# Gated-delta inverse on two stacked 64x64 diagonal blocks instead of one 128x128 block

## What is computed

```python
decay = jnp.exp(jnp.where(causal, g[..., :, None] - g[..., None, :], -jnp.inf))
Lmat = jnp.where(strict, jnp.einsum('bhncd,bhnmd->bhncm', kb, k) * decay, 0.0)
rhs = jnp.concatenate([vb, kb * jnp.exp(g)[..., None]], axis=-1)
sol = lax.linalg.triangular_solve(Lmat, rhs, left_side=True, lower=True, unit_diagonal=True)
```

## Time and profile before

| | |
|---|---|
| median of 3 runs | 4148.92 us (4146.3 to 4148.97) |
| profiled execution, its span | 4149.6 us |
| stage `gdn_core`, from the first product of level 0 to the first product of the recurrence | 348.63 to 486.24 us |
| TensorE busy over the span | 97% |

### The profile page before, as it was taken

The page is one execution under the profiler, slowest core; times in us unless marked ns, Lnnn a source line. Parts: engine busy times, 40 slices in busy tenths (PEclk is TensorE's granted clock), DMA queues, the critical chain, the costliest instruction groups (busy, mean ns, idle before and its releaser), DMA issues. The chain is left out here.

```text
span 4149.6 us, 54482 instructions
## 1 busy us (share of the span) xinstructions
PE 4030.1 (97%) x19995; PEld 3172.1 (76%) x19995; DVE 2112.4 (51%) x3948; ACT 828.9 (20%) x1835; POOL 1337.1 (32%) x1034
## 2 busy tenths in 40 slices
PE   7999999999999999999999999999999999999998
PEld 3888958887886588866688648888766787478887
DVE  3776534422553433226448535785344486357852
ACT  2432210001333200004321202111133301111110
POOL 1334304444320144421137201444311263004543
PEclk9999999999999999999999999999999999999999
DMA  7222224324440232352223231233442133313232
GB/s 241 71 61 76 61 79 130 101 86 134 126 143 21 87 91 81 87 120 60 64 60 86 74 99 51 81 91 86 96 84 64 44 88 86 84 49 91 81 86 76
DMA packets 622999, 360.81 MB, mean 87 GB/s; under 512 B 68778, under 2 KB 592331, under 8 KB 622324
## 3 DMA queue, kind: packets, MB, share of 16 engines
q1 hardware_dynamic: 607944, 335.85, 30.0%
q10 hardware_dynamic: 14892, 22.78, 1.7%
HBM read 344.41 MB, written 6.82 MB: 85 GB/s over the span
## 5 line engine op out<-in xcount | busy, mean ns | idle before, releaser
L847 PE MATMUL psum<-h_normed,weight_slot 128*128 128x256 f32 x2624 | 594.9, 380 | 0.0
L847 PEld LDWEIGHTS psum<-h_normed,weight_slot 128*128 128x128 f32 x2624 | 499.5, 190 | 69.1 <-issue 1.0
L755 POOL TENSOR_TENSOR weight_slot<-weight_slot 128x512 f32<-128x512 f32 (+1 forms) x130 | 177.2, 1363 | 886.6 <-DMA weight_slot<-in_w_ffn_in 291.6
L947 DVE COPY work<-psum 128x256 f32<-128x256 f32 x98 | 41.1, 420 | 598.2 <-PE psum L847 598.2
L3569 PE MATMUL psum<-sums_of_h,weight_slot 128*128 128x256 f32 x1280 | 282.8, 379 | 0.0
L3569 PEld LDWEIGHTS psum<-sums_of_h,weight_slot 128*128 128x128 f32 x1280 | 243.2, 190 | 33.1
L847 PE MATMUL psum<-sums_hidden,weight_slot 128*128 128x256 f32 x1056 | 244.0, 379 | 0.5 <-POOL weight_slot L761 0.3
L847 PE MATMUL psum<-sums_in,weight_slot 128*128 128x256 f32 x1008 | 231.3, 379 | 0.0
L847 PE MATMUL psum<-sums_of_h,weight_slot 128*128 128x256 f32 x960 | 221.0, 380 | 4.0 <-POOL weight_slot L761 4.0
L3569 PE MATMUL psum<-h_normed,weight_slot 128*128 128x256 f32 x960 | 217.6, 383 | 5.3 <-PEq L205 5.3
L847 PEld LDWEIGHTS psum<-sums_hidden,weight_slot 128*128 128x128 f32 x1056 | 200.3, 190 | 29.0 <-POOL weight_slot L761 2.0
(11 more groups left out here) (591 smaller groups left out, 7238.5 us busy)
## 6 DMA issues: line engine op xcount, KB each, us to landing
weight_slot<-in_w_ffn_in SPq DMA_DIRECT2D x88, 512.0 KB
weight_slot<-in_ffn_w_up SPq DMA_DIRECT2D x88, 512.0 KB
weight_slot<-in_w_gate SPq DMA_DIRECT2D x64, 512.0 KB
weight_slot<-in_w_in SPq DMA_DIRECT2D x40, 512.0 KB, 5.6
weight_slot<-in_dsw_w_in SPq DMA_DIRECT2D x36, 512.0 KB, 6.6
weight_slot<-in_gdn_w_in SPq DMA_DIRECT2D x32, 512.0 KB, 15.3
weight_slot<-in_w_ffn_out SPq DMA_DIRECT2D x64, 256.0 KB
tile_ahead<-in_w_ada SPq DMA_DIRECT2D x16, 1024.0 KB, 5.2
```

Source lines behind the costliest of these rows:

```text
L755: nc.gpsimd.tensor_tensor(b(self.S1), b(self.A21), b(self.A22), ALU.add).then_inc(self.folded, 1)
L847: last = nc.tensor.matmul(c.ps[:, 4 * bank + r // 2, (r % 2) * self.HALF:(r % 2 + 1) * self.HALF], c.slots[s][:, b * 512 + k * P:b * 512 + ...
L947: nc.vector.tensor_copy(u4, p(self.P1)).then_inc(self.link, 1)
```

## The change

Until the last level the matrices are block diagonal, with blocks of at most 64. The change stores the two diagonal 64x64 blocks of a chunk one above the other (partitions 0 to 63 and 64 to 127, 64 columns), so that T and U of a head take 256 columns each and stand side by side in one tile `tu` of 512. Every 128x128 product of levels 0 to 4 becomes a pair of 64x64 products, block 0 on partitions 0 to 63 to PSUM partitions 0 to 63 and block 1 on 64 to 127 to 64 to 127, in the same PSUM bank. Y and Z of a head go into one bank, so VectorE updates T and U with one instruction. At level 4 Y is formed for block 0 only, and U is written out in full 128x128 form, whose left half GpSimd has set to zero. Level 5 forms only the 64x64 block off the diagonal, with single 64x64 products, from `lt` without a mask, and VectorE writes its negative.

The masks have 64 columns instead of 128; masks, pairs and the result banks have four buffers instead of two. In `gdn_heads` the instruction that writes `lt` becomes two, of 64x512 and 64x256 elements. The hardware loops of levels 1 to 4 are written out. The 32 rows of side work are spread over 40 slots (slots 4 to 43) instead of 32.

```diff
-                nc.vector.tensor_tensor(st["lt"][:, ds(n, 1), :], c.ps[:, 4, :], flat, ALU.mult).then_inc(freed, 1)
+                nc.vector.tensor_tensor(near, made[0:HC, :, :], decay[0:HC, :, :], ALU.mult)
+                nc.vector.tensor_tensor(far[:, :, 0:HC], made[HC:P, :, HC:P], decay[HC:P, :, HC:P], ALU.mult).then_inc(freed, 1)
...
             def mask(i, h):
-                pool.wait_ge(x_done, i * GH + (h + 1))
-                nc.gpsimd.tensor_tensor(tiles(masked[:, h % 2, :]), tiles(st["lt"][:, h, :]),
-                                        levels[:, ds(i + 1, 1), :].to_broadcast([P, TT, P]), ALU.mult).then_inc(mask_ready, 1)
+                j = i * GH + h
+                if j >= 4:
+                    pool.wait_ge(x_done, j - 3)
+                nc.gpsimd.tensor_tensor(tiles(mask_of[h % 4]), lower[:, h, :, 0:HC],
+                                        levels[:, i + 1:i + 2, :].to_broadcast([P, TT, HC]), ALU.mult).then_inc(mask_ready, 1)
...
-                for t in range(TT):
-                    at = slice(t * P, (t + 1) * P)
-                    last = nc.tensor.matmul(c.ps[:, h % 2, at], masked[:, h % 2, at], tt[:, h, at], start=True, stop=True)
+                for t, at in enumerate(CHUNKS):
+                    if i < LAST:
+                        for b in BLOCKS:
+                            last = nc.tensor.matmul(c.ps[b, h % 2, at], mask_of[h % 4][b, at], tu[b, h, 0, at], start=True, stop=True)
+                    else:
+                        last = nc.tensor.matmul(c.ps[HC:P, h % 2, at], lower[0:HC, h, t, HC:P], tu[0:HC, h, 0, at], start=True, stop=True)
...
+                if i < LAST:
+                    for at in CHUNKS:
+                        for b in BLOCKS[0:1] if i == LAST - 1 else BLOCKS:
+                            nc.tensor.matmul(c.ps[b, bank, at], tu[b, h, 1, at], x[b, at], start=True, stop=True)
+                    for t, at in enumerate(CHUNKS):
+                        for b in BLOCKS:
+                            last = nc.tensor.matmul(c.ps[b, bank, W + t * HC:W + (t + 1) * HC], x[b, at], tu[b, h, 1, at], start=True, stop=True)
+                else:
+                    for t, at in enumerate(CHUNKS):
+                        last = nc.tensor.matmul(c.ps[0:HC, bank, at], x[HC:P, at], full[HC:P, h, t, HC:P], start=True, stop=True)
...
-                nc.vector.tensor_tensor(tt[:, h, :], tt[:, h, :], c.ps[:, 2 + h % 2, :], ALU.subtract).then_inc(t_ready, 1)
...
+                if i < LAST - 1:
+                    both = tu[:, h, :, :].rearrange("p a n -> p (a n)")
+                    nc.vector.tensor_tensor(both, both, c.ps[:, bank, :], ALU.subtract).then_inc(tu_ready, 1)
```

More of the change, by code:

```diff
@@ L82, in constant_tables @@
     levels = []
-    for lv in range(LEVELS):
-        same = (row >> (lv + 1)) == (col >> (lv + 1))
-        levels.append(same & ((col >> lv) & 1 == 1) & ((row >> lv) & 1 == 0))
-    t["levels"] = np.concatenate(levels, 1) * 1.0
+    near, far = row % HC, col[:, :HC]
+    for lv in range(LEVELS - 1):
+        same = (near >> (lv + 1)) == (far >> (lv + 1))
+        levels.append(same & ((far >> lv) & 1 == 1) & ((near >> lv) & 1 == 0))
+    t["levels"] = np.concatenate(levels + [near == far], 1) * 1.0
     t["chunkmask"] = ((row // GC == col // GC) & (row <= col)) * 1.0
@@ L1683, in head @@
                 nc.vector.tensor_tensor(st["qk"][:, ds(n, 1), :], c.ps[:, 7, :], flat, ALU.mult)
-                nc.vector.tensor_tensor(st["lt"][:, ds(n, 1), :], c.ps[:, 4, :], flat, ALU.mult).then_inc(freed, 1)
+                made = c.ps[:, 4, :].rearrange("p (t n) -> p t n", t=TT)
+                near, far = (st["lt"][half, ds(n, 1), :].rearrange("p a (t n) -> p (a t) n", t=TT) for half in (slice(0, HC), slice(HC, P)))
+                nc.vector.tensor_tensor(near, made[0:HC, :, :], decay[0:HC, :, :], ALU.mult)
+                nc.vector.tensor_tensor(far[:, :, 0:HC], made[HC:P, :, HC:P], decay[HC:P, :, HC:P], ALU.mult).then_inc(freed, 1)
             dve.wait_ge(c.x_kept, 16)
@@ L1698, in _, with gdn_core @@
             head(GH - 1, 1, False)
[L1701 removed]
+def gdn_core(c, layer, st, tu, uu):
     nc = c.nc
@@ L1726, in gdn_core @@
         LAST = LEVELS - 2
+        BLOCKS = (slice(0, HC), slice(HC, P))
+        W = TT * HC
+        CHUNKS = [slice(t * HC, (t + 1) * HC) for t in range(TT)]
+        mask_of = [masked[:, b // 2, (b % 2) * W:(b % 2 + 1) * W] for b in range(4)]
+        pair_of = [pairs[:, b // 2, (b % 2) * W:(b % 2 + 1) * W] for b in range(4)]
+        inner_of = [inner[:, b, 0:W] for b in range(2)]
+        lower = st["lt"][:, :, :].rearrange("p h (t n) -> p h t n", t=TT)
+        full = uu.rearrange("p h (t n) -> p h t n", t=TT)
+        PAIRS_AHEAD, ADA_FROM, ADA_SLOTS = 3, 4, 40
         def tiles(ap):
@@ L1765, in _ @@
                 mask(0, h)
-                if h + 3 < GH:
-                    pair(h + 3)
-            for i in range(1, LAST + 1):
+                if h + PAIRS_AHEAD < GH:
+                    pair(h + PAIRS_AHEAD)
+            for i in range(1, LAST):
                 for h in range(GH):
                     mask(i, h)
+                if i == 1:
+                    nc.gpsimd.memset(full[:, :, :, 0:HC], 0.0).then_inc(cleared, 1)
         @block.tensor
         def _(pe):
-            pe.sem_inc(x_done, 2)
             pe.sem_inc(out.done, 2)
@@ L1832, in _ @@
             turn(1)
-            for h in range(GH + 1):
-                if h < GH:
-                    inner_product(0, h, True)
-                if h >= 1:
-                    outer_products(0, h - 1, True, True)
-                if h + 2 < GH:
-                    turn(h + 2)
-            with pe.Fori(1, LAST) as i:
+            for i in range(LAST):
                 for h in range(GH + 1):
@@ L1844, in _ @@
                     if h >= 1:
-                        outer_products(i, h - 1, True, False)
+                        outer_products(i, h - 1)
+                    if i == 0 and h + 2 < GH:
+                        turn(h + 2)
             for h in range(GH + 2):
@@ L2021, in scale_row @@
                     dve.sem_inc(taken, 1)
-            for h in range(3):
+            for h in range(PAIRS_AHEAD):
                 start(h)
-            for h in range(GH):
-                if h + 3 < GH:
-                    start(h + 3)
-                level(0, h, True)
-            assert LAST - 1 == ADA_LATE and GH == KT
-            with dve.Fori(0, LAST - 1) as i:
-                for h in range(GH):
-                    level(i, h, True, 1)
-                    scale_row(i, h)
-            for h in range(GH):
-                level(LAST, h, False)
+            ROWS = KT * ADA_LATE
+            for j in range((LAST + 1) * GH):
+                i, h = j // GH, j % GH
+                if i == 0 and h + PAIRS_AHEAD < GH:
+                    start(h + PAIRS_AHEAD)
+                level(i, h)
+                j -= ADA_FROM
+                if 0 <= j < ADA_SLOTS:
+                    for r in range(j * ROWS // ADA_SLOTS, (j + 1) * ROWS // ADA_SLOTS):
+                        scale_row(r // KT, r % KT)
             at, b = 4 * (ADA_FIRST + ADA_ROWS), c.column("b_ada")
```

110 lines of the change are left out of this document (56 added, 54 removed).

## The result

The changed kernel takes 4116.61 us (median of 4 runs, 4114.11 to 4117.96), the one before 4148.38 us (4 runs, 4146.3 to 4148.97): a ratio of 0.9924 with an interval of 0.9911 to 0.9936. It is faster, by 31.8 us (0.8%), where 57 were forecast. The time lies above the range (4084 to 4109).

The account below looks back on a forecast made before the run. TensorE was taken to bound the kernel. First product to recurrence: 15.0 + 35.1 + 12.4 + 21.3 = 83.8 us against 137.6, 53.8 less; with 3.6 at the start, 57.4 gained: 4092 us, range 4084 to 4109.

Parts of the forecast that it names:

- The batch: TensorE, 64x64 products: 16 records in overlapping pairs at 0.06 us a pair, 0.48 us a batch.
- Rival B: TensorE batches: pairs don't overlap or records come no faster, 0.93 us a batch, 4144 us in all; chance 0.12.
- Levels 1 to 3 ... TensorE-bound: Levels 1 to 3: TensorE sets the pace at 1.44 us a slot, 24 slots and 0.5 making 35.1 us.
- Each half of the 1 MB loads is ... hidden: Levels 1 to 3: each half of the loads lands in 5.1 us and is used up in 7 us.
- Level 4, 12.4 us: Level 4: VectorE sets the pace at 1.55 us a slot against TensorE's 1.42; eight slots take 12.4 us.
- Rival A: Inverse: VectorE or a latency sets the pace, slots 1.6 us, 1.9 in level 4; 4103 us in all; chance 0.13.
- Level 5, 21.3 us: Level 5 and tail: single 64x64 products at 0.46 us a batch, 0.2 a slot for size changes; 21.3 instead of 26.5.
- rival C: Whole inverse: the clock falls to 1.2 GHz with the array half used and more short waits; 4168 us, slower; chance 0.04.
- Start, 3.6 us gained: Before the first product: half-size GpSimd operations and half the masks loaded bring it to 345.0; 3.6 us gained.
- The rest: The recurrence and all later stages: same work, no wait on anything that moved, zero change.

Follow-up runs that it names:

- before_unrolled: The kernel before the change with its hardware loop over levels 1 to 4 written out, nothing else: 4146.46 us, ratio 0.9998.
- one_load: The changed kernel with only the first two of the eight 1 MB loads of modulation weights: 4108.11 us, ratio 0.9903.
- warm: The changed kernel with eight dummy 128x128 products by 512 columns on TensorE before the first product with the keys: 4106.3 us, ratio 0.9895.
- split: The changed kernel with one side row a slot in levels 1 to 3, none in level 4, eight in level 5: 4108.03 us, ratio 0.9905.
- grouped: The changed kernel with each batch's four products of block 0 issued first, then block 1's four, instead of in turn: 4116.54 us, ratio 0.9925.
- loops_split: The changed kernel with the edits of loops and split together: 4097.05 us, ratio 0.9875.
- loops: The changed kernel with levels 1 to 3 in a hardware loop again and one side row in each slot of levels 1 to 4: 4109.51 us, ratio 0.9907.
- rows_early: The changed kernel with the 32 side rows in slots 4 to 35 instead of 4 to 43: 4113.8 us, ratio 0.9911.

## Why the prediction was wrong

**The batch: right.** 0.48 us was forecast from 0.06 a pair; it is 0.467. Rival B, with its 0.93 a batch, is out, and neither statement of the Trainium skill that it leaned on holds here. "TensorEngine Tiling (Array Packing)", Gotcha 1, has different row tiles not access one PSUM bank at once: here the two blocks differ in row tile, share a bank, write disjoint partitions of it, and start within 0.01 us of each other. The measurement decides: the rule as it stands is too wide for such pairs. The 62 ns a MATMUL that "TensorE: Matmul & The Clock Gate" gives for decode in microcode would be 0.99 us a batch: the trace has 0.029 us a record, so that case isn't this one.

**"Levels 1 to 3 ... TensorE-bound", 35.1 us: the step that failed first.** They take 43.3. The sum had a term for each engine and none for the code. That the loop had become straight-line code was in the diff, and I priced it at nothing, which is right for the products of before (`before_unrolled`) and wrong for the new ones beside the 1 MB loads. In `one_load` these levels take 36.5 and level 4 11.3 us; the sum's mechanism was sound once nothing holds the code up.

**"Each half of the 1 MB loads is ... hidden": half right.** No instruction waits for `w_ada`. But I asked only whether the loads come in time, not what else uses the engines while they run: the fetches of code, whose lateness is TensorE's.

**Level 4, 12.4 us: right in length by luck, and the second step that failed.** I had VectorE set the pace at 1.55 us a slot, 0.55 of it for 0.8 of a row, which at the 0.746 of the earlier trace rows is 0.60. It has 2.00 with a row in it, 0.34 + 0.84 + 0.75 and the small waits. But TensorE doesn't feel that in level 4: it has four result banks and the T and U of the pairs in hand, and goes on at 1.40. The sum spread VectorE's deficit over the eight slots; in the run it is paid at once, in level 5, where `keys` needs the newest result. The order of events at the end, from the timeline of the changed kernel:

```profile
421.85 0.75 DVE L2046 SCALAR_TENSOR_TENSOR scaled<-weight_slot,cond,scaled 128x512 f32<-128x512 f32 x1
422.76 0.41 DVE L2027 TENSOR_TENSOR weight_slot<-weight_slot,psum 64x256 f32<-64x256 f32 x1 [0.15 <-DVE scaled L2046]
423.10 0.84 DVE L2031 TENSOR_TENSOR h_normed<-weight_slot,psum 64x256 f32<-64x256 f32 x2
423.97 0.42 DVE L2034 TENSOR_SCALAR h_normed<-psum 64x256 f32<-64x256 f32 x1
424.44 1.65 PE L1846 MATMUL psum<-h_normed,keys_beta_decay 128*128 128x128 f32 x6 [2.96 <-DVE h_normed L2034]
```

VectorE is still at level 4's last pair at 423 us; line 2034, which `keys` needs, comes behind it in its queue. Rival A had VectorE as the pace of a slot; it was right on the engine and near on the pace (it said 1.9; six slots of 2.00 and two without a row of 1.29 are 1.82 on average), and wrong on where it would show.

**Level 5, 21.3 us: right at full clock, and the clock wasn't full.** The slot is 1.76 us (`warm`) where 1.79 was reckoned, and `split` has 21.8 us. In the change the stretch behind the gap is this:

```profile
424.44:434.00 9.56, 9.56 (x67) 8.53 (x68) 4.00 (x8) 2.61 (x6) 0.00 (x0) 0.50 0.01 2
...
444.00:452.71 8.71, 8.13 (x40) 7.70 (x40) 0.66 (x3) 0.98 (x2) 0.00 (x0) 0.50 1.01 274
```

0.50, 1.2 GHz, from the first `keys` to the recurrence, although TensorE is busy almost throughout: after an idle 2.96 us the clock does not come back within 28 us of single 64x64 products, full products of `keys` and one-column products. Behind the pause of 2.10 us in level 2 it was back after 3.8 us of pair batches (0.99 over 386 to 388). Which feature of the work makes the difference was not tried. That is what rival C described, at a quarter of its extent. I gave it 0.04, as a case for the whole inverse only and against "waits of tenths of a microsecond"; that one gap could switch the rest of the stage was not among the cases, and it belonged in the main forecast as soon as VectorE was over TensorE's pace in level 4. The Trainium skill ("TensorE: Matmul & The Clock Gate", on oscillation in real kernels) warns of idle gaps between stretches of dense work; this trace agrees, with its gap of 2.96 us.

**Start, 3.6 us gained: 1.4.** The head stage begins 1.2 us later in this trace than in that of before, which isn't the change's doing (it varies by 1.5 us between these traces), and the second write of `lt` costs 0.7 instead of 0.34. The masks came a little sooner than reckoned (GpSimd begins 2.9 us after their load is issued, 4.0 before). Most of the rest is a wait of 0.9 us that I did not look for. From the timeline:

```profile
340.65 5.39 PE L257 MATMUL psum<-vectors,ones 128*128 128x512 f32 x12 [0.67 <-PEq L207]
343.37 2.28 POOL L1766 TENSOR_TENSOR pairs<-l_transposed,levels 128x256 f32<-128x256 f32 x3 [41.22 <-DMA levels<-in_constants]
345.97 1.15 PE L1801 MATMUL psum<-ident,weight_slot 64*64 64x64 f32 x32
...
347.23 0.68 PE L1817 MATMUL psum<-weight_slot,masked 64*64 64x64 f32 x16
```

The products on ones, which keep TensorE at work until the masks are there, begin after the head stage, 1.2 us later than before, and the last one starts at 345.45 and runs its 0.43. VectorE has had the first pair ready since 345.06 (it begins at 344.13 and takes 0.93); TensorE takes it up at 345.97. GpSimd's chain got shorter and uncovered this one. I read it from the trace and didn't test it.

**The rest: right.** The recurrence's first 43.76 us have clock 0.90 as before 0.91, and from its start to the end nothing moved.

## What to carry to other kernels

When products get smaller, ask for the code as for data: straight-line code that costs nothing at 0.11 us a record, nor at 0.036 (`grouped`), stalls at 0.029 as soon as large loads run beside it, and a loop over the same products took half of that back. When a fast engine runs ahead of a slower one through deep buffers, the deficit isn't spread over the slots; it stands as one gap at the first full dependence, and the gap can cost a multiple of itself by the clock behind it (3 us became 12). So move side work to where the slow engine waits anyway, as `split` does, and price a gap of two microseconds or more with what comes after it.

## What the runs showed of the hardware

- Products of 64x64 in diagonally opposite places of the array, with the same bank as target, overlap fully when they alternate: 16 records in 0.467 us. In groups of one place it is 0.575 us (`grouped`), and 8 records in a single place take as long as 16 in two.
- Code comes in packets of 16 KB by a DMA queue: 18 packets in the 105 us from first product to recurrence in the change, 12 with levels 1 to 3 as a loop, 9 with level 4 in it too. A packet lasts some 3.9 us of pair batches and 14 us of the products of before. Beside a 1 MB load the next packet starts up to 7.0 us after the last, and TensorE stands still for up to 2.1 us (2.6 in `split`).
- Small products by themselves keep the clock up: it is 1.00 over 72.8 us of them in `grouped`, and over 66 us in `loops_split` with TensorE idle for 7% of the time in short pieces. It fell behind single gaps of 2 to 4 us: for about 3.8 us where pair batches followed (level 2), for all of 28 us where level 5 and its one-column products did (the change, `loops`, `rows_early`, `one_load`, `grouped`). One pause of 2.0 us in `rows_early` (404.50) had no such effect. In `split` and `loops_split`, without a gap before `keys`, it also fell in the end, at the one-column products and the wait of 1.1 us ahead of them (0.69 and 0.64 from there to the recurrence).
- VectorE's side row (line 2046) takes 0.908 us on average instead of 0.746, with single ones at 1.18 to 1.20. The change's trace shows why: of its 28 rows, the 14 that take over 0.8 us all begin while an operation of GpSimd is running, and end 0.545 to 0.548 us after that operation does:

```profile
403.37 0.73 POOL L1773 TENSOR_TENSOR masked<-l_transposed,levels 128x256 f32<-128x256 f32 x1 [1.94 <-PE psum L1817]
403.46 1.18 DVE L2046 SCALAR_TENSOR_TENSOR scaled<-weight_slot,cond,scaled 128x512 f32<-128x512 f32 x1
```

  The other 14 take at most 0.75 us; only one of them lies beside an operation that goes on, the memset of level 1. Before, the masks began 0.26 to 0.34 us after the row or later, never ahead of it, and no row took over 0.75 us. The update of line 2025, which reads PSUM, keeps its 0.69 us at 404.80 beside the mask that begins at 404.77. The dearer rows are one more reason for the backlog. No run moves the masks by themselves.
